# A four-layer transformer on one core: attention interleaved with gate products, small products moved behind input tiles

## The reference

```
mod = silu_c @ w_mod[l] + b_mod[l]          # shift, scale and gate vectors, 6 x 1024, for latent and context
a = modulate(rms_norm(h, norm1_g[l]), sh1, sc1)
p, u, vs, q, k, v, gl = jnp.split(a @ w_in[l], SPLIT_POINTS, axis=-1)
attn = neighbourhood_attention(apply_rope(to_heads(q), cos, sin), apply_rope(to_heads(k), cos, sin),
                               to_heads(v), k_ctx, v_ctx, na_rpb[l], rows)      # 8 heads of 64
mix = merge_branches(pool_mix(p, ...), sgu_mix(u, vs, ...), attn, gl, w_pool_out, w_sgu_out, w_attn_out, w_o)
h = h + g1 * mix
h = h + g2 * sq_relu_mlp(modulate(rms_norm(h, norm2_g[l]), sh2, sc2), w_ff1[l], w_ff2[l])

def merge_branches(pool_o, sgu_o, attn_o, gate_logits, w_po, w_so, w_ao, w_o):
    gp, gs, ga = jnp.split(jax.nn.sigmoid(gate_logits), N_BRANCH, axis=-1)
    y = gp * (pool_o @ w_po) + gs * (sgu_o @ w_so) + ga * (attn_o @ w_ao)
    return y @ w_o
```

## Time and profile before

| | |
|---|---|
| median of 3 runs | 2565.59 us (2559.14 to 2566.82) |
| profiled execution, its time | 2566.31 us |
| its span in the trace | 2564.5 us |
| PE busy | 2369.6 us, 92% |
| DVE busy | 1678.8 us, 65% |
| ACT busy | 899.3 us, 35% |
| POOL busy | 579.6 us, 23% |
| read from HBM | 334.89 MB, mean 131 GB/s over the span |

### The profile page before, as it was taken

How to read it: one execution, slowest core, us unless ns; L and a number is a source line. 1 busy time by engine, 2 the same in 40 slices (tenths; PEclk the granted TensorE clock), 3 DMA queues, 4 the chain that set the end, 5 groups by cost and what they waited for, 6 DMA issues and landing times.

```text
span 2564.5 us, 31653 instructions
## 1 busy us (share of the span) xinstructions
PE 2369.6 (92%) x12640; PEld 1948.0 (76%) x12640; DVE 1678.8 (65%) x2533; ACT 899.3 (35%) x1331; POOL 579.6 (23%) x386
## 2 busy tenths in 40 slices
PE   5989999999999998989988999887999999898998
PEld 4874688778888794889988796446788887747997
DVE  6776765696666566888994434655866666487444
ACT  1312433332333332444434423442322333243444
POOL 3001000232345301003365000004222444002244
PEclk9997999999999997999999998668999999889999
DMA  8530244345544460566755131001465444402652
GB/s 279 164 131 1 75 130 140 116 164 195 182 155 135 147 217 1 172 215 199 254 196 171 60 99 50 1 1 50 148 197 183 156 140 109 112 1 83 181 179 85
DMA packets 268979, 337.99 MB, mean 132 GB/s; under 512 B 31000, under 2 KB 185504, under 8 KB 268448
## 3 DMA queue, kind: packets, MB, share of 16 engines
q1 hardware_dynamic: 268832, 335.97, 41.0%
HBM read 334.89 MB, written 1.05 MB: 131 GB/s over the span
## 4 chain that ended last, share of the span: by engine, by line
PE 78%; DVE 14%; ACT 3%; issue 3%; POOL 2%; DMA 1%; SPq 0%; DVEq 0%; POOLq 0%; ACTq 0%
PE PS L601 22%; PE PS L603 22%; PE PS L602 22%; DVE bias L1271 3%; PE PS L772 2%; DVE w_l L1250 2%; PE PS L798 1%; PE PS L669 1%; DVE nmax L1462 1%; PE PS L914 1%; PE PS L893 1%; PE PS L883 1%; PE PS L785 1%; POOL a_l L1727 1%; DVE scr L1476 1%
## 5 line engine op out<-in xcount | busy, mean ns | idle before, releaser
L601 PE MATMUL PS<-a_h,w_h 128*128 128x512 f32 (+1 forms) x2832 | 983.8, 347 | 51.4 <-DVE a_l L1375 26.1
L602 PE MATMUL PS<-a_l,w_h 128*128 128x512 f32 (+1 forms) x2832 | 974.2, 344 | 0.0
L603 PE MATMUL PS<-a_h,w_l 128*128 128x512 f32 (+1 forms) x2832 | 973.7, 344 | 0.0
L1250 DVE TENSOR_TENSOR w_l<-ring,w_h 128x1024 fp32r<-128x1024 f32 x426 | 548.2, 1329 | 311.6 <-ACT w_h L983 308.6
L601 PEld LDWEIGHTS PS<-a_h,w_h 128*128 128x128 f32 x2832 | 544.9, 192 | 126.1 <-issue 34.3
L983 ACT ACTIVATE w_h<-ring 128x1024 fp32r<-128x1024 f32 x426 | 426.5, 1051 | 571.3 <-PE PS L603 513.2
L603 PEld LDWEIGHTS PS<-a_h,w_l 128*128 128x128 f32 x2832 | 545.0, 192 | 61.6
L602 PEld LDWEIGHTS PS<-a_l,w_h 128*128 128x128 f32 x2832 | 545.7, 193 | 59.9 <-issue 0.2
L1271 DVE SCALAR_TENSOR_TENSOR bias<-ring,silu,bias 128x512 f32<-128x512 f32 x532 | 469.3, 937 | 4.4 <-DMA ring<-in_w_mod 0.5
L1727 POOL TENSOR_TENSOR a_l<-hid,a_h 128x2048 fp32r<-128x2048 f32 (+1 forms) x60 | 222.7, 3712 | 247.8 <-ACT a_h L999 247.8
L1746 POOL TENSOR_TENSOR hid<-hid 128x256 f32<-128x256 f32 (+1 forms) x128 | 151.1, 1182 | 430.7 <-ACT hid L965 430.7
(11 more groups left out here) (168 smaller groups left out, 2464.3 us busy)
## 6 DMA issues: line engine op xcount, KB each, us to landing
ring<-in_w_ff SPq DMA_DIRECT2D x64, 1024.0 KB, 5.4
ring<-in_ffn_w SPq DMA_DIRECT2D x64, 1024.0 KB, 5.4
ring<-in_w_mod SPq DMA_DIRECT2D x48, 1024.0 KB, 5.1
ring<-in_ada_w SPq DMA_DIRECT2D x48, 1024.0 KB, 5.2
ring<-in_w_in SPq DMA_DIRECT2D x42, 1024.0 KB, 5.6
...
```

Source lines behind the costliest of these rows:

```text
L601: nc.tensor.matmul(out, stat[0], mov[0], start=start, stop=False, **kw)
L602: nc.tensor.matmul(out, stat[0], mov[1], start=False, stop=False, **kw)
L603: return nc.tensor.matmul(out, stat[1], mov[0], start=False, stop=stop, **kw)
L1250: V.tensor_tensor(w_l[:, n % 2, c], ring[:, split_raw[n] % SLOTS, c], w_h[:, n % 2, c].bitcast(F32), ALU.subtract).then_inc(s_wl, 1)
```

## The change

Of the plan (`make_plan`), the core:

```diff
+    small = {4: (("pool", 0), ("pool", 1)), 5: (("wp", 0), ("wp", 1), ("rope", 0), ("rope", 1)),
+             6: (("rope", 2), ("rope", 3), ("sgu", 0), ("sgu", 1)), 7: (("rope", 4), ("rope", 5)),
+             8: (("rope", 6), ("rope", 7))}
-                  mods=blocks(0, 4, 8) if l == 0 else blocks(2, 0, 2), every=1 + l, skip=1, **base)
+            phase("b1_in", tiles=(nt, 2, nt, 2, 2, 2, 2, 4, 4), extra=small,
+                  mods=blocks(0, 4, 6) if l == 0 else (), at=(1, 2, 7, 8), **base)
-            phase("rope", units=8, chunks=8, **base)
-            phase("pool_sgu", units=6, **base)
-            heads = [("lat", h) for h in range(8)] + ([("ctx", h) for h in range(8)] if l == 0 else [])
-            phase("attn", heads=heads, **base)
+            heads = ([("ctx", h) for h in range(8)] if l == 0 else []) + [("lat", h) for h in range(8)]
+            phase("mix", tiles=(2, 2, 4) * 4 + (2,), halves=(2, 5, 8, 11), banks=(0, 1, 2), heads=heads, **base)
-            phase("merge", tiles=(6, 2, 2, 2) * 4, splits=KC, mods=blocks(0, 8, 12) if l == 0 else blocks(2, 2, 6),
-                  every=2, **base)
-            phase("to_h", tiles=(2,) * 4, src="y", gate=2, name="w_o", **base)
+            phase("post", tiles=(2, 2, 2, 4, 4), splits=KC, mods=blocks(0, 6, 8) if l == 0 else (), heads=heads, **base)
+            phase("to_h", tiles=(2,) * 4, src="y", gate=2, name="w_o", mods=blocks(0, 8, 10) if l == 0 else (), **base)
-            phase("m_in", tiles=(4,) + (2,) * 4 + (4,) * 4 + (2,) * 4, **base)
+            phase("m_in", tiles=(4,) + (2,) * 4 + (4,) * 4 + (2,) * 4, mods=blocks(2, 4, 8), at=range(1, 9), **base)
-            phase("to_h", tiles=(2,) * 4, src="a", gate=2, name="m_out", **base)
+            phase("to_h", tiles=(2,) * 4, src="a", gate=2, name="m_out", mods=blocks(2, 8, 10), **base)
-        in_ff1, in_ff2 = {0: (blocks(1, 0, 8), blocks(1, 8, 12)), 1: (blocks(2, 6, 10), blocks(2, 10, 12)),
-                          2: (blocks(3, 0, 8), blocks(3, 8, 12)), 3: ((), ())}[layer]
+        in_ff1, at1, in_ff2, at2 = {
+            0: (blocks(0, 10, 12) + blocks(1, 0, 6), range(16), blocks(1, 6, 12) + blocks(2, 0, 2), range(16)),
+            1: (blocks(2, 2, 4), range(0, 16, 4), (), ()),
+            2: (blocks(2, 10, 12) + blocks(3, 0, 6), range(16), blocks(3, 6, 12), range(12)),
+            3: ((), (), (), ())}[layer]
```

A block in `blocks` is two mods. On PE, the bias of sgu is one matmul over all tokens for each half instead of one for each token tile, and the new phase mix does head by head:

```diff
+                    for half in range(2):
+                        g = 2 * i + half
+                        nc.tensor.matmul(out[HD * half:HD * half + HD, 0:cols].rearrange("p (t n) -> p t n", t=nt),
+                                         ident[0:4, g:g + 1].broadcast_to([4, HD]),
+                                         aux[0:4, A_SB:A_SB + P].unsqueeze(1).broadcast_to([4, nt, P]),
+                                         start=True, stop=False, skip_group_check=True)
...
+                        def dense(j):
+
+                            g, r = divmod(j, per)
+                            if per == 4:
+                                gates(steps[3 * g + r // 2], (r % 2,))
+                            else:
+                                gates(steps[3 * g + r], (0, 1))
+                            if r == per - 1:
+                                branches(steps[3 * g + 2])
...
+                        for i in range(n):
+                            if i >= 1:
+                                values(i - 1, ph["head"])
+                            turn(i)
+                            if i + 1 < n:
+                                scores(i + 1)
+                                dense(i + 1)
```

```diff
+                        if i >= 1:
+                            out(i - 1)
+                        probs_t(i)
+                        if i + 1 < n:
+                            rowmax(i + 1)
+                        if per == 4 and r == 0:
+                            split_w(s0 + 3 * g + 1)
+                        if r == per - 3 or (per == 2 and r == 0):
+                            split_w(s0 + 3 * g + 2)
+                        if i + 1 < n:
+                            inverse(i + 1)
```

More of the change, by code:

```diff
@@ L62, in make_plan, with add_units, phase @@
     hunits = []
-    n = dict(s=0, u=0, x=0, norm=0, sq=0, sq7=0, head=0, mu=0, final=0, y=0)
-    def phase(kind, tiles=(), units=0, mods=(), per=1, every=1, skip=0, splits=0, **kw):
-        ph = dict(kind=kind, norm=n["norm"], head=n["head"], x=n["x"], y=n["y"], s=n["s"], u=n["u"], mu=n["mu"], **kw)
+    bank_of, nth = [], []
+    n = dict(s=0, u=0, x=0, norm=0, sq=0, sq7=0, head=0, mu=0, turn=0)
+    used = [0] * 4
+    def add_units(count, banks):
+        for _ in range(count):
+            b = banks[n["turn"] % len(banks)]
+            n["turn"] += 1
+            bank_of.append(b)
+            nth.append(used[b])
+            used[b] += 1
+            n["u"] += 1
+    def phase(kind, tiles=(), units=0, mods=(), per=1, at=None, splits=0, extra=None, banks=(0, 1, 2, 3), halves=(), **kw):
+        ph = dict(kind=kind, norm=n["norm"], head=n["head"], x=n["x"], s=n["s"], u=n["u"], mu=n["mu"], **kw)
         mods = list(mods)
@@ L69, in phase @@
         for i, e in enumerate(tiles):
-            st = dict(s=n["s"] if e is not None else None, u=n["u"], units=e or 0, mods=[], modu=None)
+            st = dict(s=n["s"] if e is not None else None, u=n["u"], units=e or 0, mods=[], modu=None,
+                      half=i in halves, extra=(extra or {}).get(i, ()))
             n["s"] += e is not None
-            n["u"] += e or 0
-            if i >= skip and i % every == 0:
+            add_units((e or 0) + len(st["extra"]), banks)
+            if at is None or i in at:
                 st["mods"], mods = mods[:per], mods[per:]
@@ L79, in phase @@
         assert not mods
-        n["u"] += units
+        add_units(units, banks)
         n["x"] += splits
@@ L135, in make_plan @@
         n["norm"] += 1
[L137 to L140 removed]
+        in_ff1, at1, in_ff2, at2 = {
[3 more added lines that the diff above has]
+            3: ((), (), (), ())}[layer]
+        phase("ff1", tiles=(2,) * 16, mods=in_ff1, at=at1, **base)
+        phase("to_h", tiles=((0,) * 7 + (4,)) * 2, splits=16, mods=in_ff2, at=at2, src="ff", gate=5, name="ff2", **base)
         if l == 1:
@@ L710, in _ @@
                             else:
-                                fm(st, u + j, w, slice(P * j, P * j + P), PA, ALL if i >= 5 else cols)
+                                fm(st, u + j, w, slice(P * j, P * j + P), from_a, ALL if i >= 5 else cols)
+                        if i == 4:
+                            pe.wait_ge(s_aux, AUX_LANDED[ph["layer"]])
+                            wait_units(pe, ph["steps"][1]["u"])
+                        for e, (what, j) in enumerate(st["extra"]):
+                            small_unit(ph, u + st["units"] + e, what, j)
                         mod_unit(st)
@@ L1094, in _ @@
                     nc.scalar.preload_act_table_set(LN_EXP)
+                    for c in range(4, KC):
+                        round_y(c)
                 elif kind == "attn":
@@ L1443, in _ @@
+                        rotate(ph, u + c, c)
                 elif kind == "attn":
@@ L1775, in mask_bias, with add_sgu @@
                         ins.then_inc(s_bias, 1)
-                    if ph["block"] == 0:
-                        wait_units(pool, u)
-                        pool.wait_ge(s_aux, AUX_LANDED[ph["layer"]])
-                        pool.wait_ge(s_winld, 32 * (ph["l"] + 1))
-                        for i in range(8):
-                            mask_bias(i)
+                    def add_sgu(c):
+                        wait_unit(pool, ph["steps"][3 * (c // 2) + 2]["u"] + 2 * (c % 2) + 1)
+                        y = yT[:, c, 0:cols]
+                        nc.gpsimd.tensor_tensor(y, y, gate[:, 2 + c % 2, 0:cols], ALU.add).then_inc(s_ys, 1)
+                    pool.wait_ge(s_mcsum, ph["mu"])
+                    pool.wait_ge(s_aux, AUX_LANDED[ph["layer"]])
+                    pool.wait_ge(s_winld, 32 * (ph["l"] + 1))
+                    mask_bias(lat0)
+                    mask_bias(lat0 + 1)
+                    for i in range(-1, n):
+                        if lat0 + 2 <= i + 3 < n:
+                            mask_bias(i + 3)
+                        if i >= 0 and i % per == per - 2:
+                            add_sgu(2 * (i // per))
+                            add_sgu(2 * (i // per) + 1)
+                elif kind == "post":
+                    for c in range(4):
+                        wait_unit(pool, ph["steps"][3]["u"] + c)
+                        pool.wait_ge(s_ys, KC * ph["l"] + c + 1)
+                        y = yT[:, c, 0:cols]
+                        nc.gpsimd.tensor_tensor(y, y, gate_a[:, c, 0:cols], ALU.add).then_inc(s_y03, 1)
                 elif kind == "m_heads":
```

574 lines of the change are left out of this document (388 added, 186 removed).

## The result

The changed kernel takes 2495.11 us, median of four runs (2487.17 to 2495.83), against 2566.2 (2559.14 to 2568.03) of the kernel before beside it. The ratio is 0.9721, with a 95% interval of 0.9694 to 0.9748: faster by 71 us. Forecast were 2502 and 2465 to 2534. The profiled execution has a span of 2493.5 us against 2564.5.

What follows compares the result with a forecast made beforehand. PE is busy 92% of the span, so gains must come where it is idle, slow or follows another engine. 110 us won less 46 lost is 64: 2564.5 - 64 + 1.8 = 2502 us, range 2465 to 2534.

Steps and rivals of the forecast that it cites:

- Part 1: Layers 0 and 1: small products placed behind b1_in tiles lose their waits and the low clock; 34 us won.
- part 3: b1_in of layer 0: one inverse root for all token tiles, a step earlier, ends DVE's wait for ACT; 5 us won.
- Part 2: Mixes of layers 0 and 1: attention between gate products, each head's chain hidden behind 7.3 us of cover; 25 us won.
- the forecast's worst case: Mix heads: a split beside POOL stands in the chain, making it 8.4 us against 7.3 of cover.
- Part 4: Layer 1: merge, ff1 and ff2 freed of mods run at PE's full pace, post loses 2; 41 us won.
- Part 5: Mods moved into w_o and ff2 of layer 0, m_in, m_out and ff2 of layer 2; 38 us lost, bounds 12 to 68.
- second item: w_o of layer 0: handover from post and the norm that follows late cost 5 us more.
- Part 6: Handovers in the mixes: first scores, last values, tanh before its bank is free, halves of half-size tiles; 8 us lost.
- mods hidden: Rival: at the mods' new places only transposes cost, 12 us instead of 38, giving 2476 us; chance 0.17.
- waits in mix: Rival: PE waits 1.25 us more in each of 24 heads, 30 us, giving 2532 us; chance 0.12.
- blocking by POOL: Rival: POOL and DVE block each other throughout at the mods' new places, the bound of 68, giving 2532 us; chance 0.10.
- the clock stayed at 1.00 in mix: Rival: the clock falls in mix as in the attention before, costing 40 us, giving 2542 us; chance 0.08.

Runs made afterwards that it cites:

- Two experiments: Changed kernel with all small products at the end of b1_in, 2506.73 us; changed kernel with the sgu bias in its old form, 2511.77 us.
- one more reduction: Changed kernel with extra row maxima on DVE in each of the 24 mix heads: one more, 2494.0 us; three more, 2529.78 us.
- the kernel with the mods back: Changed kernel with layer 2's modulation back in layer 1's b1_in, post, ff1 and ff2: 2510.24 us against 2496.41 of the changed kernel.

## Why the prediction was right, and where its terms were off

The time came out 7 us below the forecast and well inside its range, by the mechanisms that it named. That it is as near as 7 us is in part luck. Layer 1's attention and merge won 5.5 us more than their terms, w_o of layer 0 lost 5.7 less, and layer 3 won 3.5 without a term; against them, the heads of layer 2 lost 6.5 without a term, and ff2 of layer 0 3.8 more than its term.

Part 1 (34 for the small products) was split rightly in kind: the first rows of the stage table show 29.6 and 14.1 us for layers 0 and 1, with part 3 and the transposes in them, against 26 and 17. Two experiments take it apart: place 16 us, form of the bias 18, each edit made alone. The forecast took 5.5 us for sgu between 4.9 and 9.8 by the row of pool, and it takes 4.1. What it missed is that the clock falls beside the old bias.

Part 2 (25) held: PE doesn't wait in either mix, one more reduction is hidden, three are not. The cover is 7.5 us for the 7.3 forecast. The chain was added up less well. It is 4.8 us without a split for the 4.2 of the forecast, and a whole split lengthens it by 1.4 us, to 6.2, not by its whole 2.35, since part of it lies in DVE's wait for ACT. POOL did prolong some splits in the chain, 2.86 instead of 2.35 us above, but the 8.4 us of the forecast's worst case didn't come.

Part 3 (5) was read wrongly in one point: DVE waits 5.17 us for ACT's inverse root only ahead of the first token tile, and 0.60 ahead of each of the other three. The second token tile's row on DVE, and the wait of PE in b1_in of layer 0, in the kernel before:

```profile
128.23 0.35 DVE L1399 TENSOR_SCALAR scr<-scr,lnst 128x256 f32<-128x256 f32 x1 [0.60 <-ACT lnst L970]
```

```profile
PE PS L601 <- DVE w_l L1250: 4.6, 1, 4.6
```

The term held all the same: PE waits 4.6 us for a split, once, and in the changed kernel it doesn't wait in b1_in. No run takes this edit alone.

Part 4 (41 for layer 1) held: the feed-forward won 23.1 for the 24 forecast, and the kernel with the mods back loses 39 in layer 1 as a whole.

Part 5 (38) was right in sum for what it named, 6.8 + 1.0 + 14.8 + 3.4 + 6.8 + 1.7 = 34.5, but w_o was mis-sized. The step from "a tile is 10 to 16 us on DVE against 10.9" to an excess of 7.5 us failed: no product of w_o waited, since a split is a tile ahead. The loss is 1.8 us of transposes, 3.5 more of waiting for the late squares, and 1.6 of the norm's products at the lower clock; the forecast had the late norm as its second item, at 5. In ff2 of layer 0, where PE waits 5.8 us ahead of the norm (0.7 before) and 4.5 for splits, the term of 11 was too small. Six operations of one mod there took 10.20 us where they take 4.06 alone: 6.1 more where the row gave 4.6, with POOL's squares on top of its rests. The next mod took 9.74 for 5.4, 4.3 more, as the row gave.

Part 6 (8 for handovers) is the term most off. Mix and post of layer 0 are 238.8 us; 177.8 for the gate products with their transposes, less 1.7, and 58.8 of attention give 234.9, and 4 are left. They aren't a wait: the 24 products behind the scores take 5.7 us, from 329.2 to 334.9, where the full pace gives 5.45, and all sixteen such groups lose 0.2 to 0.3. In layer 1 all but nothing is left: 92.3 + 39.2 = 131.5 against 132.2. I took 8 from a wait that there wasn't, and PE shows none for a bank either, with three instead of four.

Not forecast were 6.5 us in the heads of layer 2, which the change leaves alone. They carry the same instructions at a lower granted clock, 0.59 instead of 0.63, and differ by 10 us among kernels that have them alike. So one profiled execution doesn't tell what a change does there. What makes the clock differ from one execution to the next stays open: thirteen traces show 172.6 to 182.8 us, with mods in m_in (172.6, 176.5 and 182.7 among them) and without (172.9 and 180.6). Layer 3's 3.5 us are of the same kind as far as the trace shows: the granted clock in its attention is 0.80 over 60 us instead of 0.74.

Of the rivals, mods hidden and waits in mix are refuted by the traces; blocking by POOL is there, at a part of its bound; the clock stayed at 1.00 in mix.
